# Last projection of a two-layer trunk: merged branches stationary, gated weight rows moving, residual kept by tokens

## The reference, cut to what matters

```python
def _layer(x, mod, norm_w, w_in, ...):
    shift, scale, gate = jnp.split(mod, 3, axis=-1)            # mod = silu(c) @ w_ada[l] + b_ada[l]
    h = _rmsnorm(x, norm_w) * (1.0 + scale[:, None]) + shift[:, None]
    proj = h @ w_in
    ...
    merged = (g[:, :, 0] * (ya @ w_pa) + g[:, :, 1] * (yb @ w_pb) + g[:, :, 2] * (yc @ w_pc)).astype(x.dtype)
    return x + gate[:, None] * (merged @ w_out)
# after the last layer: _rmsnorm(x, final_norm_w)
```

## Time and profile before

| | us |
|---|---|
| median of 3 runs (1147.16 to 1148.03) | 1147.76 |
| the profiled execution's own time | 1147.11 |
| its span in the trace | 1145.4 |
| PE busy in the span | 1125.6 |
| DVE, POOL, ACT busy | 655.1, 558.9, 525.4 |

### The profile page before, as it was taken

The page is one execution under the profiler, slowest core; times in us unless marked ns, Lnnn a source line. Parts: engine busy times, 40 slices in busy tenths (PEclk is TensorE's granted clock), DMA queues, the critical chain, the costliest instruction groups (busy, mean ns, idle before and its releaser), DMA issues.

```text
span 1145.4 us, 15393 instructions
## 1 busy us (share of the span) xinstructions
PE 1125.6 (98%) x5930; PEld 929.4 (81%) x5930; DVE 655.1 (57%) x804; ACT 525.4 (46%) x908; POOL 558.9 (49%) x404
## 2 busy tenths in 40 slices
PE   6999999999999999999999999999999999999997
PEld 6778888888888878888898888888788888788886
DVE  5716465669887545437360635655988853132275
ACT  5544266655445533223543535666545553332333
POOL 5535444445535546455913363445535544555551
PEclk7999999999999999999999999999999999999999
DMA  9656423235442455653304563233542524333332
GB/s 322 203 118 202 137 75 92 75 110 138 120 121 75 131 178 159 206 161 110 95 21 106 152 187 90 74 84 111 135 118 71 139 64 110 92 111 92 92 101 84
DMA packets 217226, 139.23 MB, mean 122 GB/s; under 512 B 11929, under 2 KB 207553, under 8 KB 217153
## 3 DMA queue, kind: packets, MB, share of 16 engines
q1 hardware_dynamic: 216504, 137.59, 41.7%
...
q10 hardware_dynamic: 648, 0.66, 0.2%
...
## 4 chain that ended last, share of the span: by engine, by line
PE 89%; POOL 4%; DVE 3%; DMA 1%; ACT 1%; SPq 1%; issue 0%; DVEq 0%; ACTq 0%; POOLq 0%
PE main L629 76%; PE psC L629 4%; PE psA L629 3%; POOL w_lo L555 3%; PE psB L629 3%; DMA raw<-in_w_in 1%; PE psB L847 1%; PE psB L827 1%; POOL y_lo L555 0%; ACT w_hi L1034 0%; SPq L370 0%; DVE h_lo L1435 0%; DVE psC L1389 0%; DVE tmp L1511 0%; DVE tmp L1502 0%
## 5 line engine op out<-in xcount | busy, mean ns | idle before, releaser
L555 POOL TENSOR_TENSOR w_lo<-raw,w_hi 128x512 fp32r<-128x512 f32 x344 | 509.8, 1503 | 541.2 <-ACT w_hi L1034 540.9
L629 PE MATMUL main<-h_hi,w_hi 128*128 128x512 f32 (+1 forms) x1104 | 436.6, 396 | 3.6 <-ACT h_hi L1034 2.3
L629 PE MATMUL main<-h_hi,w_lo 128*128 128x512 f32 (+1 forms) x1104 | 426.4, 387 | 0.0
L629 PE MATMUL main<-h_lo,w_hi 128*128 128x512 f32 (+1 forms) x1104 | 426.2, 387 | 0.0
L1034 ACT ACTIVATE w_hi<-raw 128x512 fp32r<-128x512 f32 x344 | 199.5, 623 | 302.2 <-PE main L629 208.6
L629 PEld LDWEIGHTS main<-h_hi,w_hi 128*128 128x128 f32 x1104 | 207.4, 188 | 56.2 <-issue 11.1
L629 PEld LDWEIGHTS main<-h_hi,w_lo 128*128 128x128 f32 x1104 | 207.6, 188 | 43.1
L629 PEld LDWEIGHTS main<-h_lo,w_hi 128*128 128x128 f32 x1104 | 207.6, 188 | 41.3 <-issue 1.9
L1709 DVE TENSOR_TENSOR tmp<-main,misc 128x512 f32<-128x512 f32 x32 | 22.1, 691 | 169.3 <-PE main L629 169.3
L1555 DVE SCALAR_TENSOR_TENSOR misc<-main,cols,misc 128x511 f32<-128x511 f32 (+2 forms) x96 | 71.9, 749 | 61.1 <-ACT misc L1034 58.5
L629 PE MATMUL main<-y_hi,w_hi 128*128 128x512 f32 x256 | 100.5, 393 | 0.0
(11 more groups left out here) (256 smaller groups left out, 1252.0 us busy)
## 6 DMA issues: line engine op xcount, KB each, us to landing
raw<-in_w_in SPq DMA_DIRECT2D x124, 512.0 KB, 3.9
xbc<-in_w_ada SPq DMA_DIRECT2D x16, 512.0 KB, 4.8
zs<-in_w_ada SPq DMA_DIRECT2D x16, 512.0 KB, 4.4
raw<-in_w_pc SPq DMA_DIRECT2D x16, 512.0 KB, 3.8
raw<-in_w_out SPq DMA_DIRECT2D x16, 512.0 KB, 3.7
zs<-in_w_ada SPq DMA_DIRECT2D x16, 256.0 KB, 7.3
xbc<-in_w_in SPq DMA_DIRECT2D x8, 512.0 KB, 7.4
big<-in_w_ada SPq DMA_DIRECT2D x16, 256.0 KB, 7.3
```

What stands on the lines that cost most here:

```text
L555: nc.gpsimd.tensor_tensor(lo_b[:, cut, :], raw_b[:, cut, :], hi_b[:, cut, :].bitcast(F32), ALU.subtract).then_inc(s_split[b], 2 * BT_ // kt)
L629: return nc.tensor.matmul(o, a, b_, start=start, stop=stop)
```

## The change

Three parts, in both layers:

1. x stays as tokens by channels (`x_tok[P, PAIRS, D]`, 128 tokens on partitions, four token blocks t). The transposed x exists for layer 0's start only.
2. The last projection turns round: the stationary operand is a 128x128 block of `merged` (channels k, tokens t), the moving one half a row block of `w_out` (512 of the 1024 columns). Rows k = 0 to 7 are the outer loop, and all eight PSUM halves (t, half) are open at once. SP loads row blocks (`load_out`). The gate is now a multiplication of the row block by a row of 1024 values on all partitions (`gate_out`, two DVE operations for each k), so the gate is written to memory and read back as a broadcast row. x + product is `add_out`, the squares are summed by ACT along its free axis, and no matmul of ones or spreading is needed.
3. For layer 1 DVE and ACT scale x's rows by the root (`xn`, in `zs`), PE transposes these (`turn`, 32 blocks of 128x128), and DVE reads the transposed rows from PSUM (`turned_32`). At the very end POOL multiplies by the final norm's weight, as a broadcast row, and DVE and ACT scale by the root; the transposes back are gone.

The diff, cut to its core and shifted left; `norm_of` and `evac_count` only count semaphores, `turned(k)` is the PSUM place of transposed block k, and removed functions that the section above describes are left out:

```diff
-xT = sb("xT", [P, KT, SEQ])
+x_tok = sb("x_tok", [P, PAIRS, D])
...
+gate_row = nc.dram_tensor("gate_row", [D], F32).ap()
...
-sum_sq = buf_b
+xT = xbc[:, 0:KT, :]
+xn = zs[:, :, :].rearrange("p a b -> p (a b)").rearrange("p (t n) -> p t n", n=D)
+out_gate = buf_w
+out_norm = zs[:, 0:2, :].rearrange("p a b -> p (a b)")
...
+out_ps = [(psA[:, 0:512], psA[:, 512:1024]), (psC0, psC1), (main[0][:, :], main[1][:, :]),
+          (psB[:, 0:512], psB[:, 512:1024])]
...
+    def load_out(l, k):
+        u, b = U_OUT + k // 2, k % 2
+        sp.wait_ge(s_split[b], halves_before(l, u))
+        sp.dma_start(raw[:, b, :, :].rearrange("p k n -> p (k n)"), w_out[l, k * P:(k + 1) * P, :]
+                     ).then_inc(s_raw[b], 16)
...
+                sp.wait_ge(s_gm, 4 * (l + 1))
+                with nc.allow_non_contiguous_dma("one row of 1024 values"):
+                    sp.dma_start(gate_row.rearrange("(k p) -> p k", p=P), gmul[:, :]).then_inc(s_grw, 16)
...
+            if m == 0:
+                sp.wait_ge(s_grw, (l + 1) * 16)
+                sp.wait_ge(s_yu, (l + 1) * PAIRS)
+                sp.dma_start(out_gate, gate_row.unsqueeze(0).broadcast_to([P, D])).then_inc(s_gr, 16)
+            if (l, m) == (DEPTH - 1, 1):
+                sp.wait_ge(s_yz, DEPTH * PAIRS)
+                sp.dma_start(out_norm, final_norm_w.unsqueeze(0).broadcast_to([P, D])).then_inc(s_fw, 16)
+        for k in range(KT):
+            load_out(l, k)
...
-            split_pre(0)
...
-            split_pre(1)
...
+        section(l, U_C, U_OUT - U_C)
+        for k in range(KT):
+            split_half(l, U_OUT + k // 2, k % 2, 0)
+            if l == 0 and k == KT - 1:
+                split_pre(KT - 2)
+            split_half(l, U_OUT + k // 2, k % 2, 1)
+            if l == 0 and k > 0:
+                split_pre(k - 1 if k < KT - 1 else k)
+    l = DEPTH - 1
+    pool.wait_ge(s_fw, 16)
+    for t, half in np.ndindex(PAIRS, 2):
+        if (t, half) != (0, 1):
+            pool.wait_ge(s_evac[half], evac_count(l, t))
+            nc.gpsimd.tensor_tensor(stage_x[:, t, cols_of(half)], x_tok[:, t, cols_of(half)],
+                                    out_norm[:, cols_of(half)], ALU.mult).then_inc(s_u, 1)
...
+    def out_product(l, k, t, half):
+        b, tok = k % 2, slice(t * P, (t + 1) * P)
+        cut = slice(half * BT_, (half + 1) * BT_)
+        ps = out_ps[t][half]
+        mm(ps, h_hi[:, k, tok], w_hi[:, b, cut, :], k == 0, False)
+        mm(ps, h_hi[:, k, tok], w_lo[:, b, cut, :], False, False)
+        return mm(ps, h_lo[:, k, tok], w_hi[:, b, cut, :], False, k == KT - 1)
+    def out_ready(l, k, half):
+        u, b = U_OUT + k // 2, k % 2
+        pe.wait_ge(s_split[b], part_count(l, u, half, b))
+        pe.wait_ge(s_mh, l * KT + k + 1)
+        pe.wait_ge(s_m, l * KT + k + 1)
+    def out_rows(l, k):
+        order = np.ndindex(PAIRS, 2) if k < KT - 3 else ((t, half) for half in range(2) for t in range(PAIRS))
+        for half in range(2):
+            out_ready(l, k, half)
+        for t, half in order:
+            if (k, t) == (0, 2):
+                pe.wait_ge(s_evac[half], l * COUPLES + U_OUT)
+            if (k, t, half) == (0, 3, 0) and l + 1 < DEPTH:
+                pe.wait_ge(s_unf, 8)
+            last = out_product(l, k, t, half)
+            if (k, t, half) == (KT - 3, PAIRS - 1, 0):
+                last.then_inc(s_first, 1)
+        last.then_inc(s_tile[k % 2], 1)
+    def out_end(l, ks, t, half):
+        for k in ks:
+            out_ready(l, k, half)
+            last = out_product(l, k, t, half)
+            if (t, half) == (PAIRS - 1, 1):
+                last.then_inc(s_tile[k % 2], 1)
+            elif k == KT - 1:
+                last.then_inc(s_outp[half], 1)
+    def turn(t, ks, done=False):
+        for k in ks:
+            last = nc.tensor.transpose(turned(k)[:, t % 2 * P:(t % 2 + 1) * P], xn[:, t, k * P:(k + 1) * P],
+                                       ident[:, :])
+        if done:
+            last.then_inc(s_xnT, 1)
...
+            four = [(0, 0, main[0]), (0, 1, main[1]), (1, 0, psB[:, 0:512]), (1, 1, psB[:, 512:1024])]
+            def four_high(half, k, these):
+                tok = tokens(half)
+                pe.wait_ge(s_hhi, h_count(l, k, half))
+                for u, b, ps in these:
+                    if (half, k) == (0, 0):
+                        pe.wait_ge(s_evac[b], l * COUPLES - 1 + u)
+                    pe.wait_ge(s_splitw, 4 * u + 2 * b + k // BT_ + 1)
...
+            def four_low(half, k, these):
+                tok = tokens(half)
+                pe.wait_ge(s_h, h_count(l, k, half))
...
             for half in range(2):
...
                 for k in range(KT):
...
-                        sum_squares(l - 1, 1, psC1)
...
-                        spread(psC1, rms, 2 * l + 1, range(2, PAIRS))
+                    for these in ((four[:3], four[3:]) if (half, k) == (0, 0) else (four,)):
+                        four_high(half, k, these)
+                        four_low(half, k, these)
+                    if (half, k) in ((0, KT - 3), (0, KT - 1)):
...
+                        pe.wait_ge(s_xn, PAIRS)
+                        pe.wait_ge(s_h32, h_count(l, first + BT_ - 1, 0))
+                        turn(2, range(first, first + BT_))
+                        turn(3, range(first, first + BT_), True)
...
-        for k0, k1 in ((0, KT - 2), (KT - 2, KT)):
...
-                out_part(l, b, k0, k1)
...
-                h_tile(l, u, b)
...
+        for k in range(KT - 2):
+            out_rows(l, k)
+        for k in range(KT - 2, KT):
+            for t in range(2):
+                for half in range(2):
+                    out_end(l, (k,), t, half)
+        for half in range(2):
+            out_end(l, range(KT - 2, KT), 2, half)
+        if l + 1 < DEPTH:
+            pe.wait_ge(s_evac[0], evac_count(l, 1))
+            pe.wait_ge(s_evac[1], evac_count(l, 1))
+            pe.wait_ge(s_xn, 1)
+            pe.wait_ge(s_xnd, 1)
+            turn(0, range(KT))
+        out_end(l, range(KT - 2, KT), 3, 0)
+        if l + 1 < DEPTH:
+            pe.wait_ge(s_xn, 2)
+            pe.wait_ge(s_xnd, 2)
+            turn(1, range(BT_), True)
+            turn(1, range(BT_, KT), True)
+        out_end(l, range(KT - 2, KT), 3, 1)
...
+        if u >= U_OUT:
+            act.wait_ge(s_gw[b], l * KT + 2 * (u - U_OUT) + half + 1)
+        else:
+            wait_raw(act, l, u, b, half)
...
+        for k in range(1, KT - 1):
+            if k > 1:
+                w_hi_part(l, U_OUT + k // 2, k % 2)
+            if l == 0:
+                pre_hi(k - 1)
+        w_hi_half(l, COUPLES - 1, 1, 0, free=(s_first, l + 1))
+        if l == 0:
+            pre_hi(KT - 2)
+        w_hi_half(l, COUPLES - 1, 1, 1)
+        if l == 0:
+            pre_hi(KT - 1)
+        f(sm[:, 0, 0:1], eps[:, 0:1], ACT.Sqrt)
+        square(l, 0, 0)
+        square(l, 0, 1)
+        square(l, 1, 0)
         if l + 1 < DEPTH:
...
+            seed(rms, norm_of(l, 0), slice(0, 1))
+            square(l, 1, 1)
+            x_norm(0, cols_of(0))
+            seed(rms, norm_of(l, 1), slice(1, 2))
+            square(l, 2, 0)
+            x_norm(1, cols_of(0))
...
+    l = DEPTH - 1
+    square(l, 1, 1)
+    seed(rms, norm_of(l, 0), slice(0, 2))
+    square(l, 2, 0)
+    square(l, 2, 1)
+    seed(rms, norm_of(l, 2), slice(2, 3))
+    act.wait_ge(s_xnd, 3)
+    x_final(0, slice(0, D), 1, s_fc[0])
+    square(l, 3, 0)
+    square(l, 3, 1)
+    seed(rms, norm_of(l, 3), slice(3, 4))
+    x_final(2, slice(0, D), 5, s_fc[2])
+    x_final(3, cols_of(0), 6, s_xn)
+    act.wait_ge(s_xn, PAIRS + 1)
...
+    def add_out(l, t, half):
+        if (t, half) == (PAIRS - 1, 1):
+            dve.wait_ge(s_tile[1], (l + 1) * COUPLES)
+        else:
+            dve.wait_ge(s_outp[half], l * (PAIRS - half) + t + 1)
+        tt(x_tok[:, t, cols_of(half)], x_tok[:, t, cols_of(half)], out_ps[t][half], ALU.add
+           ).then_inc(s_evac[half], 1)
+    def mean_out(l, t0, t1):
+        dve.wait_ge(s_sq, l * 2 * PAIRS + 2 * t1)
+        stt(q_mean[:, t0:t1], sm[:, 4, t0:t1], EPS, sm[:, 4, PAIRS + t0:PAIRS + t1], ALU.add, ALU.add
+            ).then_inc(rms[0], 1)
+    def x_norm(t):
+        dve.wait_ge(rms[2], norm_of(0, t))
+        dve.wait_ge(s_evac[1], evac_count(0, t))
+        ts_(xn[:, t, cols_of(1)], x_tok[:, t, cols_of(1)], q_inv[:, t:t + 1], None, ALU.mult).then_inc(s_xnd, 1)
...
+            def turned_32(half, k):
+                tok = tokens(half)
+                dve.wait_ge(s_xnT, 2 * half + k // BT_ + 1)
+                if k >= 4:
+                    dve.wait_ge(s_h, h_count(l, k - 4, half))
+                ts_(h_tmp[k % 4][:, tok], turned(k), mod[:, l, KT + k:KT + k + 1], mod[:, l, k:k + 1], ALU.mult,
+                    ALU.add).then_inc(s_h32, 1)
+            def turned_low(half, k):
+                tok = tokens(half)
+                dve.wait_ge(s_hhi, h_count(l, k, half))
```

(145 more changed lines are left out.)

294 lines of the change are left out of this document (74 added, 220 removed).

## The result

The changed kernel takes **1154.2 us** (median of 4 runs, 1152.4 to 1156.7), the one before 1147.9 (1147.2 to 1148.1): a ratio of 1.0059, 95% interval 1.0046 to 1.0071. It is 6.3 us slower, where 1146.7 and at most 1150.5 were forecast. The profiled execution is the longest of the four, 1156.66 us with a span of 1154.9; its runs scatter over 4 us, those of before over 1.

The account below looks back on a forecast made before the run. PE, busy 98% of the span, was taken as the bound. Span 1145.4 + 3.4 (first stretch) - 4.5 (second and third) = 1144.3; execution 1146.0; median 0.65 above, so 1146.7 us, range 1142.0 to 1150.5.

Parts of the forecast that it names:

- Moved DMAs: Gate row's write ahead of w_pa's load, its read-back, and the other moved loads: all hidden, cost 0.
- slow write: Rival, chance 0.04: the gate row's write lasts 9.6 us and makes ACT 4.1 late in each layer; 1153.8 us.
- First stretch: Layer 0's last projection to the end of layer 1's four opening tiles: 70.2 plus waits 5.05, 75.25 us, +3.4.
- the fold: Layer 0's projection: DVE's fold, behind two new operations, ends at 535.5 where PE needs it at 535.45; wait 0.3 us.
- psB: Layer 0's projection: this bank is free at 540.4, PE asks for it at 539.9; wait 0.7 us.
- row 2: Layer 0's projection: this row's operands are ready at 547.6 against 547.4; wait 0.4 us.
- row 4: Layer 0's projection: behind 13 two-input DVE operations, ready at 560.7, PE done with row 3 at 558.7; wait 2.3 us.
- row 7: Layer 0's projection: this row's second half waits behind row 6's splits and two `split_pre`; 0.85 us.
- The mechanism of turns: Layer 0's projection: two-input DVE operations and POOL's go in turns, about 1.77 us for one of each, 0.66 alone.
- POOL kept out: Rival, chance 0.10: DVE keeps the port, row 2 is 4.8 late; +2.4 in layer 0, +3.4 in layer 1; 1152.5 us.
- Second stretch: Layer 1's last projection: 43.5 us instead of 47.49, -4.0, with waits of 0.
- Third stretch: From PE's last product to the span's end: 8.5 us against 9.05.

Follow-up runs that it names:

- e4: Changed kernel with the gate row's write issued some 85 us earlier, plus row 4's gating ahead of rows 5 to 7's low parts in DVE's queue: 1148.3 us.
- e3: Changed kernel with the gate row's write issued some 85 us earlier, plus one-column root and mean operations taking a per-partition scalar as second operand: 1149.36 us.

## Why the prediction was wrong, step by step

- **Moved DMAs: wrong, and the step that failed.** I set the write at 0, because w_pa's load had 5.5 us of cover and a *read* of 64-byte runs landed in 3.8. The nearest row was the wrong kind. Isolated, the write costs 11.0 us; in the changed kernel's median 4.8 of the 7.5 us between forecast and result. The rival "slow write" had a time of 1153.8, and I gave it 4 in 100. That this lies near 1154.2 is luck. Its write lasts 9.6 where 13.1 was measured, and its path was wrong: I looked at what is queued *behind* the write (w_pa, ACT late); what decided was a transfer *ahead* of it, already in flight, whose landing doubled, and whose reader has no cover. And I had no price for the clock.
- **First stretch: +3.4 forecast, +4.5 measured, by two errors of opposite sign.** The waits came to 3.8 us (76.38 less 72.57), not 5.05: 0.45 for the fold (0.3), 0.41 for psB (0.7), none at row 2 (0.4), 0.83 at row 4 (2.3), 0.40 at row 7 (0.85), none before the first transposes and the fourth tile (0.3 each), and two that I hadn't listed, 0.77 for the last merge and 0.93 for row 1's low part. But PE was busy for 72.57, where I had counted 70.2: a matmul's pitch (0.2267, start to start) holds inside a run of its kind, and this stretch has many starts. The two tiny sums take 0.64 besides their wait (0.14 in the sum); the first product behind a wait or a transpose is 0.30 to 0.34 from the next; and the last one ahead of a wait counts as busy for its whole 0.39.
- **The mechanism of turns: right in kind, rarer than laid out.** The maxima of `gate_out` (1.79) and `merged_lo` (1.81) are turns of 1.77. `merged_lo`'s median is 1.78. But `gate_out`'s is 0.68, where one above 0.69 was to be the sign, and POOL's splits for rows 1 to 7 have a mean of 1.47, not near 1.6. Even so row 4 was ready 26.9 us from the stretch's start, 1.6 later than laid out; its wait is short because PE, held up before it, also came 2.8 later. e4 shows that the order of DVE's queue set this wait.
- **POOL kept out: wrong.** Row 2, where it should have cost 4.8, has no wait.
- **Second stretch: right**, 43.52 against 43.5, no wait of PE.
- **Third stretch: mis-sized**, 11.0 against 8.5. I had the chain, and priced its root at 0.2 for each small operation. Beside POOL two of them took 0.44 and 1.19 and the mean of t = 2 took 0.74; e3 took 1.4 us out of the tail by their form alone. `add_out(3, 1)` ends 3.2 behind PE (forecast 2.0) and the last scaling 7.2 (forecast 4.8). From there to the end it is 3.9, forecast 3.7: the writes are not the error.
- Without the write, then, the sum would have said 1146.7 for a kernel that takes 1149.4: inside the range, outside the sum's own 1144.8 to 1148.8, and with the wrong sign against before.
- Three sums of the prediction don't come out of their own terms, and none changes the outcome: the seven waits of the first stretch add up to 5.15, not 5.05; 4.1 us in each layer for the slow write give 1154.9, not 1153.8; and POOL kept out gives 4.4 less 2.3, 2.1 instead of 2.4, in layer 0.
